# Two-slab products of 512 columns in the up and down stages, and down products in two passes of eight tiles

## The reference

```python
def conv_ffn(h, w_up, conv_w, conv_b, w_down):          # w_up 2048 x 11264, w_down 5632 x 2048
    u = causal_dwconv(h @ w_up, conv_w, conv_b)         # three taps along the tokens
    g, val = jnp.split(u, 2, axis=-1)
    return (jax.nn.silu(g) * val) @ w_down
...
x = x + gate_f * conv_ffn(h, w_up, conv_ffn_w, conv_ffn_b, w_down)
```

## Time and profile before

| | us |
|---|---|
| median of three runs | 2589.81 (2589.5 to 2592.26) |
| the profiled execution | 2596.39 |
| its span, first to last instruction | 2594.7 |
| PE busy | 2421.5 (93% of the span) |
| DVE busy | 1869.9 (72%) |
| ACT busy | 1129.7 (44%) |
| granted PE clock, mean | 0.97 of 2.4 GHz |
| moved by DMA | 615.73 MB, 237 GB/s |

### The profile page before, as it was taken

The page is one execution under the profiler, slowest core; times in us unless marked ns, Lnnn a source line. Parts: engine busy times, 40 slices in busy tenths (PEclk is TensorE's granted clock), DMA queues, the critical chain, the costliest instruction groups (busy, mean ns, idle before and its releaser), DMA issues.

```text
span 2594.7 us, 51150 instructions
## 1 busy us (share of the span) xinstructions
PE 2421.5 (93%) x21498; PEld 2357.6 (91%) x21498; DVE 1869.9 (72%) x2202; ACT 1129.7 (44%) x1246; POOL 96.1 (4%) x184
## 2 busy tenths in 40 slices
PE   4899958899999999999899889999999999999997
PEld 4899848799999999999799788888999999999997
DVE  6988878888777677777788666668877554555645
ACT  3344363355543334443543344433554443344433
POOL 0020000000000000000000000000000000000000
PEclk8999979899999999999999999899999999999999
DMA  8988947777778877779478122218576455555552
GB/s 356 421 333 320 352 160 270 281 267 263 281 284 308 327 277 265 284 275 344 176 272 320 67 89 97 97 65 308 213 281 250 178 181 192 178 179 183 188 212 97
DMA packets 88526, 615.73 MB, mean 237 GB/s; under 512 B 9656, under 2 KB 13264, under 8 KB 14928
## 3 DMA queue, kind: packets, MB, share of 16 engines
q1 hardware_dynamic: 65216, 445.07, 45.9%
q0 software_dynamic: 23184, 168.83, 17.2%
HBM read 609.64 MB, written 4.22 MB: 237 GB/s over the span
## 4 chain that ended last, share of the span: by engine, by line
PE 74%; DVE 14%; DMA 5%; ACT 5%; issue 2%; SPq 0%; DVEq 0%; POOLq 0%; ACTq 0%
PE ps L742 22%; PE ps L744 22%; PE ps L743 22%; DMA ada_raw<-in_ada_stream 3%; DVE ada_raw L1651 2%; DVE first_raw L1651 2%; DVE w_lo L1639 2%; DVE w_lo L1635 1%; DMA first_raw<-in_ada_stream 1%; ACT w_hi L1109 1%; PE ps L628 1%; DMA w_raw<-in_w_stream 1%; PE ps L654 1%; DVE xbc L1786 1%; PE ps L779 1%
## 5 line engine op out<-in xcount | busy, mean ns | idle before, releaser
L742 PE MATMUL ps<-h_hi,w_hi 128*128 128x256 f32 x4480 | 1284.6, 287 | 78.6 <-DVE h_lo L1767 34.1
L743 PE MATMUL ps<-h_lo,w_hi 128*128 128x256 f32 x4480 | 1275.5, 285 | 0.0
L744 PE MATMUL ps<-h_hi,w_lo 128*128 128x256 f32 x4480 | 1274.8, 285 | 0.0
L742 PEld LDWEIGHTS ps<-h_hi,w_hi 128*128 128x128 f32 x4480 | 867.8, 194 | 89.7 <-DVE h_lo L1767 36.1
L1635 DVE TENSOR_TENSOR w_lo<-w_raw,w_hi 128x2048 fp32r<-128x2048 f32 x297 | 678.8, 2288 | 309.9 <-ACT w_hi L1103 309.6
L743 PEld LDWEIGHTS ps<-h_lo,w_hi 128*128 128x128 f32 x4480 | 868.0, 194 | 0.5
L744 PEld LDWEIGHTS ps<-h_hi,w_lo 128*128 128x128 f32 x4480 | 867.8, 194 | 0.0
L1103 ACT CAST w_hi<-w_raw 128x2048 fp32r<-128x2048 f32 x298 | 567.6, 1908 | 678.0 <-DMA w_raw<-in_w_stream 665.7
L1651 DVE SCALAR_TENSOR_TENSOR ada_raw<-ada_raw,ada_c 128x2048 f32<-128x2048 f32 x160 | 365.3, 2285 | 42.6 <-DMA ada_raw<-in_ada_stream 42.4
L742 PE MATMUL ps<-hid_hi,w_hi 128*128 (+1 forms) x1344 | 377.3, 281 | 7.1 <-DVE w_lo L1635 5.5
L744 PE MATMUL ps<-hid_hi,w_lo 128*128 (+1 forms) x1344 | 375.7, 280 | 0.0
(11 more groups left out here) (353 smaller groups left out, 1581.4 us busy)
## 6 DMA issues: line engine op xcount, KB each, us to landing
w_raw<-in_w_stream SPq DMA_DIRECT2D x372, 1024.0 KB, 5.3
ada_raw<-in_ada_stream POOLq DMA_DIRECT2D x160, 1024.0 KB, 7.2
first_raw<-in_ada_stream SPq DMA_DIRECT2D x32, 1024.0 KB, 10.1
kept_raw<-in_w_stream SPq DMA_DIRECT2D x4, 1024.0 KB, 9.4
x<-in_x_t SPq DMA_DIRECT2D x1, 2048.0 KB, 9.9
cs_b<-cs_rows SPq DMA_DIRECT2D x4, 512.0 KB, 6.8
x_kept<-x SPq DMA_DIRECT2D x1, 2048.0 KB, 14.7
out_t<-x SPq DMA_DIRECT2D x4, 512.0 KB, 2.7
```

Source lines behind the costliest of these rows:

```text
L742: mm(o, hi, r_hi, start=first, stop=False, **kw)
L743: mm(o, hi, r_lo, start=False, stop=False, **kw)
L744: return mm(o, lo, r_hi, start=False, stop=last, **kw)
```

## The change

The two halves of an activation become slabs of one tensor (`h_both`, `hid_both`). A new helper `wide` replaces `three` in the up and down stages: one matmul of the high weights with both slabs, 512 columns, fills the whole bank (hi*hi left, hi*lo right), and a second one of the low weights with the high slab, 256 columns, adds lo*hi to the right half. Whoever reads a result must add the two halves of a bank. In the up stages, ACT first copies the four right halves to `tmp` (`small`), DVE adds the left halves (`add`) and both give the banks back; the taps read `tmp`. One step more stands in each chunk's order.

A down output tile now fills a bank, so eight of the 16 tiles fit, and the down product runs in two passes. A unit is two k-tiles (256 rows) by 1024 columns (`_down_units`, laid out on the host). Eight tiles are ended in the middle of the stage and eight at its end, bank by bank (`down_tile`), and DVE adds each to `x` in two steps, left and right half (`down_add`). The squares of the first eight tiles follow the middle of the second down stage. In the first down stage one ada sum goes with each of the units 2 to 10 and 15 to 23; in the second one the counts stand in the call. PE's loop over the down units is unrolled. The diff, cut to its core (the helpers replaced stand above; the calls of the second block are changed alike, and the order of buffers in SBUF too):

```diff
+            sb(under, "before_prob_t_a", [P, KT, T])
             prob_t_a = sb(under, "prob_t", [P, 4, 384])
-        h_lo = sb(ctx, "h_lo", [P, KT, T], F32R)
+        h_both = sb(ctx, "h_both", [P, 2, KT, T], F32R)
+        h_hi, h_lo = h_both[:, 0], h_both[:, 1]
...
+            hid_both = sb(s, "hid_both", [P, 2, 2 * FFN_A, T], F32R)
+            hid_hi, hid_lo = hid_both[:, 0], hid_both[:, 1]
...
+
+            first = 4 * (e_next % 2)
+            return [(first + j) % 8 for j in range(8)]
...
+            def wide(b, hi, lo, k, first, both=h_both, big=h_hi):
+                mm(ps[:, b, :].rearrange("p (a t) -> p a t", a=2), hi, both[:, :, k], start=first, stop=False,
+                   skip_group_check=True)
+                return mm(ps[:, b, T:512], lo, big[:, k], start=False, stop=False, skip_group_check=True)
...
-                        elif kind == "cols" and added is not None and i == 0:
+                        elif kind == "wide" and added is not None and i == 0:
                             for j in range(4):
-                                pe.wait_ge(down_evac, added + j + 1)
+                                pe.wait_ge(down_out, 16 * added + 8 + j + 1)
                                 for k in range(4):
                                     w = slice(k * 512 + j * P, k * 512 + j * P + P)
-                                    last = three(bank(4 * par_ + j), w_h[:, w], w_l[:, w], h_hi[:, k], h_lo[:, k],
-                                                 k == 0, False)
+                                    last = wide(4 * par_ + j, w_h[:, w], w_l[:, w], k, k == 0)
...
+            def down(d, u0, hc0, e_next, n, name=None):
...
+                banks, per = down_banks(e_next), n // 2
...
+                def tile(b, w_h, w_l, f0, first):
+                    for f in range(2):
+                        w = slice(f * 1024 + b * P, f * 1024 + b * P + P)
+                        last = wide(b, w_h[:, w], w_l[:, w], f0 + f, first and f == 0, hid_both, hid_hi)
+                    return last
+
...
-                                         hid_lo[:, i], i == 0 and j % 2 == 0, False, skip_group_check=True)
+                    for q in range(2):
+                        pe.wait_ge(hid_lo_s, hc0 + q + 1)
+                        w_h, w_l = weights(q)
+                        for b in banks[4 * half:4 * half + 4]:
...
-                with pe.Fori(1, n // 4 - (name is not None)) as b:
-                    body(b)
+                for q in range(2, n):
...
+                    w_h, w_l = weights(q)
+                    for k, b in enumerate(banks):
+                        if q == per:
+                            pe.wait_ge(down_out, 16 * d + k + 1)
+                        last = tile(b, w_h, w_l, f0, q == per)
+                        if q in (per - 1, n - 1):
+                            last.then_inc(down_tile, 1)
+                        if q == per and k == 0:
+                            pe.wait_ge(down_tile, 16 * d + 8)
+                            pe.nop().then_inc(units_used, 1)
+                    if q == n - 1:
+                        pe.wait_ge(down_tile, 16 * d + 16)
+                        pe.nop().then_inc(units_used, 1)
+                    elif q != per - 1:
+                        last.then_inc(units_used, 1)
...
             def sums(name, n):
...
+                def small(c, par_):
+                    chunk_done(c, u0)
+                    nc.scalar.copy(tmp[:], ps[:, 4 * par_:4 * par_ + 4, T:512]).then_inc(act_evac, 1)
+
                 def taps(c, par_):
-                    chunk_done(c, u0)
+                    act.wait_ge(dve_evac, c + (e0 + 3))
                     for i in range(4):
                         o = 16 * c + 4 * i + 16 * (hc0 % (FFN_A + FFN_B))
-                        last = A(conv_y[:, par_, i], bank(4 * par_ + i), ACT.Identity, bias=pc(par_name, o + 3),
+                        last = A(conv_y[:, par_, i], tmp[:, i], ACT.Identity, bias=pc(par_name, o + 3),
                                  scale=pc(par_name, o + 2))
-                    last.then_inc(act_evac, 1)
+                    last.then_inc(S("conv_open"), 1)
...
+                    if u_next is not None:
+                        hi_unit(u_next)
+                        hi_unit(u_next + 1)
+                    for k in range(8, 16):
+                        down_squares(d, name, joint, k, banks[k - 8])
...
+                def up(c, par_):
+                    lo(c, 0, u0)
+                    lo(c, 1, u0)
+                    evac[0](c - 1, 1 - par_)
+                    some_ada(c, 2, (par_ - e0) % 2)
+                    lo(c, 2, u0)
+                    evac[1](c - 1, 1 - par_)
+                    some_ada(c, 3, (par_ - e0) % 2)
+                    evac[2](c - 1, 1 - par_)
+                    lo(c, 3, u0)
+                    evac[3](c - 1, 1 - par_)
...
+                def add(c, par_):
+                    dve.wait_ge(act_evac, c + (e0 + 3))
+                    tt(tmp[:], ps[:, 4 * par_:4 * par_ + 4, 0:T], tmp[:], ALU.add).then_inc(dve_evac, 1)
+
                 def taps(c, par_):
-                    dve.wait_ge(act_evac, c + (e0 + 3))
+                    dve.wait_ge(S("conv_open"), c + (hc0 + 1))
...
-                            last = stt(out=conv_y[:, par_, i, d:T], in0=ps[:, 4 * par_ + i, 0:T - d],
+                            last = stt(out=conv_y[:, par_, i, d:T], in0=tmp[:, i, 0:T - d],
...
+            def down_add(d, gate0, k, banks):
+                for e in (k, k + 1):
+                    dve.wait_ge(down_tile, 16 * d + e + 1)
+                    b = banks[e % 8]
+                    j = 8 * (e // 8) + b
+                    stt(out=x[:, j], in0=ps[:, b, 0:T], scalar=mod[:, gate0 + j:gate0 + j + 1], in1=x[:, j], op0=ALU.mult,
+                        op1=ALU.add).then_inc(down_half, 1)
+                for e in (k, k + 1):
+                    dve.wait_ge(down_half, 16 * d + e + 1)
+                    b = banks[e % 8]
+                    j = 8 * (e // 8) + b
+                    stt(out=x[:, j], in0=ps[:, b, T:512], scalar=mod[:, gate0 + j:gate0 + j + 1], in1=x[:, j], op0=ALU.mult,
+                        op1=ALU.add).then_inc(down_out, 1)
...
+            def down(d, u0, n, gate0, p0, products, e_next, u_next=None, name=None, joint=0):
+                banks, per = down_banks(e_next), n // 2
+                pair = p0
+                for q in range(2, n - 2 if name is not None else n):
+                    if name is not None and q >= n - 4:
+                        lo_kept(name, q - n + 4)
+                    if q == per + 1:
+                        for k in range(0, 8, 2):
+                            down_add(d, gate0, k, banks)
+                    lo_unit(u0 + q)
+                    if name is not None and per + 2 <= q < per + 6:
+                        for k in (2 * (q - per - 2), 2 * (q - per - 2) + 1):
+                            if k:
+                                add_square(name, joint, k)
+                    if q in products:
+                        for _ in range(products[q]):
+                            ada(pair, pair % 2)
+                            pair += 1
...
+                elif u_next is not None:
+                    lo_unit(u_next)
+                for k in range(8, 16, 2):
+                    if name is not None and u_next is not None and k == 12:
+                        lo_unit(u_next + 1)
+                    down_add(d, gate0, k, banks)
+                    if name is not None:
+                        for e in (k - 2, k - 1):
+                            if e >= 8:
+                                add_square(name, joint, e)
+                if name is None:
+                    lo(0, 1, u_next)
+                dve.wait_ge(down_out, 16 * d + 16)
...
+                if pairs:
+                    ada(2 * c + (98 - 18), 0)
                 lo(c, 2, U_UP1A)
                 ev[1](c - 1, 1 - par_)
                 if pairs:
-                    ada(2 * c + (98 - 18), 0)
+                    ada(2 * c + (99 - 18), 1)
+                ev[2](c - 1, 1 - par_)
                 lo(c, 3, U_UP1A)
-                ev[2](c - 1, 1 - par_)
-                if pairs:
-                    ada(2 * c + (99 - 18), 1)
+                ev[3](c - 1, 1 - par_)
...
+            mod_bias(GATE_F, KT)
+            down(0, U_DN1A, 2 * FFN_A, GATE_F, 104, {**{q: 1 for q in range(2, 11)}, **{q: 1 for q in range(15, 24)}}, UP1B, U_UP1B)
...
+            down(1, U_DN1B, 2 * FFN_B, GATE_F, 142, {2: 1, 3: 2, 4: 1, 5: 1, 6: 1, 7: 1, 8: 1, 14: 1, 15: 1, 16: 1, 17: 1}, C_LORA, U_LORA,
+                 "mid", 2)
...
+            steps.link(ts(mu1[:], pcol("mu", 0, 27), -1.0, 1.0, ALU.mult, ALU.add))
+            dve.nop().then_inc(S("mu1"), 1)
...
 
+def _down_units(w):
+
+    k, n = w.shape
```

272 lines of the change are left out of this document (103 added, 169 removed).

## The result

The changed kernel takes 2577.9 us (median of 9 runs, 2567.5 to 2588.6) where the kernel before, run beside it, takes 2592.3 (2587.3 to 2597.5): ratio 0.9946, 95% interval 0.9924 to 0.9967, some 14 us faster. The forecast was 32.3 us faster, 2557.5 us: the sign is right and the time lies in the range, but less than half of the gain came. The profiled execution took 2577.89 us, span 2576.2.

A forecast was written before the change was run, and what follows sets the result against it. TensorE (PE), busy 93% of the span, was taken to bound the kernel. Gains of 49.1 us less losses of 16.8 gave net 32.3, from 2589.8 to 2557.5 us; range 2543 to 2584.

The forecast's parts named there:

- Part 1: Up and down products: two matmuls replace three, 0.3468 us an up pair; 37.2 us gained up, 7.3 down.
- rival d: Down stages: the short matmul spacing stays with wide matmuls, giving 2550 us; chance 0.15.
- Rival (a): Up and down products: the two-slab operand costs like two matmuls, 0.2400 us; slower, 2601.5 us; chance 0.06.
- Rival (a'): Only part of the third matmul's cost is saved, wide steps about 0.2344 us; no change, 2590 us; chance 0.03.
- Part 2: Up chunks' longer hand-over: low weights still arrive in time, slack 1.2 us; nothing lost.
- rival (b): Up chunks with ada sums: DVE becomes the bound, up to 26 us per us short, 2583.5 us; chance 0.11.
- Part 3: Four hand-overs from up to down: PE waits longer for unit 2's low weights, 2.5 us each, 9.9 lost.
- Part 4: Down stages in two passes: bank additions hidden, some stalls go, while ada loads, tails and moved constants cost time.
- The start of the next up stage: Behind the first down stages: the wait of 1.3 us, twice, shrinks to some 0.4; 1.8 us gained.
- The ada loads: Down stages: denser loads cost 1 us in the first and 3 us in the second, bounds 0 and 10.
- Rival (c): Down stages: the ada loads hold them back by 10 us instead of 4, giving 2564 us; chance 0.10.
- Tails: Ends of the second down stages: PE waits longer for DVE's additions and squares before the sums; 2.4 us lost.

The follow-up runs named there:

- contiguous: The changed kernel with the two slabs interleaved, so the 512 moving columns lie in one piece; 2572.6 us, ratio 0.9914 to the kernel before.
- split512: The changed kernel with each 512-column matmul issued as two of 256 columns, a weight load each; 2606.0 us, ratio 1.0042 to the kernel before.
- early_spread: early_unit with the eight ada sums of the second down stage's first half given one to a unit; 2561.5 us, ratio 0.9883.
- early_unit: The changed kernel with the next down stage's unit 2 weights (high and low) made ahead of the last up chunk's product; 2566.4 us, ratio 0.9891.
- bank_runs: early_spread with an up unit's pairs ordered four in a row into one bank, then the next bank; 2562.8 us, ratio 0.9888.
- up_only_early: up_only with unit 2's high and low weights for the next down stage made ahead of the product; 2564.0 us, ratio 0.9891.
- after: The changed kernel itself, in its first measurement and profile; 2577.9 us, ratio 0.9946 to the kernel before.
- after_again: The changed kernel without any edit, run once more with a new profile; 2576.5 us, ratio 0.9932 to the kernel before.
- small_first: The changed kernel with each pair's matmuls in the other order, 256 columns first and 512 after; 2575.2 us, ratio 0.9924.
- k_outer: The changed kernel with the first weight unit of both second up stages done row tile by row tile; 2581.1 us, ratio 0.9952.
- up_only: The kernel before with wide matmuls in the up products alone, down stages as they were; 2570.5 us, ratio 0.9924.

## Why the prediction was right or wrong

**Part 1, the pair: mechanism right, size off.** The step that failed is "A new pair takes 0.2268 + 0.1200 = 0.3468 us", priced at 37.2 us over the up stages: these saved 26.3 where 36.7 were forecast. I took it from one short stretch of matmuls all of one size and one pace of 256-column matmuls, and asked only for the two-slab operand's cost, bounded from 0.2268 to 0.2400. A mixed stream has two paces, and the long one costs 0.8 us in the first and 4.3 in each second up stage: 9.4 of the 11.8 us missing. That the short pace meets 0.3468 is in part luck: it is made of 0.230 and 0.117, two terms that are off in opposite directions. And the prediction's own sign of being wrong, a wide step above 0.23, did come: in the long pace the wide steps are 233 to 241 ns, 237 in the mean. The earlier trace rows had shown 256-column matmuls at 0.1163 to 0.1175 beside 0.1200; I noted that the cause of it was not visible and bounded only a gain from it (rival d), where it called for a loss as well.

Rival (a) is out by contiguous and split512. Rival (a'), wide steps of about 0.2344 and no gain at all, is out as to the time; but as to the pair it is what the long pace is, 0.3533 against its 0.3544, and half of the third matmul's cost was saved there. The Trainium skill's gap of N/2.4 + 2.5 ns ("TensorE: Matmul & The Clock Gate", Back-to-back issue gap), which the page gives for a matmul without a budget for its weight load and by which a third matmul costs 2.5 ns, does not agree with this stream, where every matmul has a load: between split512 and the unedited kernel 32 us lie on 4224 triples, 7.6 ns each. In the down stages the pair took 346.7 against 350.0 to 353.3, some 8.0 us where I had 7.3.

**Part 2, no stall in the up chunks: right but for one step.** In the chunk that starts at 628.5 us the low weights of unit 3 come from 641.54:

```profile
629.78 1.23 DVE L1974 TENSOR_TENSOR tmp<-ps,tmp 128x1024 f32<-128x1024 f32 x1 [1.84 <-ACT tmp L1308]
...
641.54 2.28 DVE L1656 TENSOR_TENSOR w_lo<-w_raw,w_hi 128x2048 fp32r<-128x2048 f32 x1
```

They end 15.3 us after the boundary (walked: 15.4), and the addition takes 1.23 (estimated: 1.22). At one chunk boundary the low weights were late, behind two ada sums in a row:

```profile
715.24 4.49 DVE L1656 TENSOR_TENSOR w_lo<-w_raw,w_hi 128x2048 fp32r<-128x2048 f32 x2
...
717.58 0.50 PE L750 MATMUL ps<-h_both,w_hi 128*128 128x512 f32 x1
```

That step took 0.41 us in place of 0.12; the first of the two subtractions in DVE's row ends at about 717.5, and early_spread's row of this place, shown above, names the wait. A wait for low weights inside the up chunks was named as a sign of being wrong; here it is 0.3 us, once. As the cost that rival (b) meant it is out. The rival's price was set for 26 chunks with two ada sums; the trace has 30 (24, 20 and 16 sums in three stages), so a us too little in each would have cost 30.

**Part 3, the junction: the place and the wait right, the cost too small, for what follows the stall was left out.** Forecast 2.5 us each. PE after, at the second down stage:

```profile
1160.05 0.28 PE L752 MATMUL ps<-hid_both,w_lo 128*128 128x256 f32 x1
1163.46 0.47 PE L750 MATMUL ps<-hid_both,w_hi 128*128 128x512 f32 x1 [3.13 <-DVE w_lo L1660]
...
1165.06 0.63 PE L750 MATMUL ps<-hid_both,w_hi 128*128 128x512 f32 x1
...
1165.70 0.63 PE L750 MATMUL ps<-hid_both,w_hi 128*128 128x512 f32 x1
```

From 1160.05 to 1163.46 are 3.41 us in place of 0.12; before, such a step was 0.61 to 0.66. So 2.7 us each, 11.0 in all against 9.9. But from 1164.7 to 1168.2 the granted clock is at 1.2 GHz: a pair takes 0.64 instead of 0.35, and 3.4 us of that cost 1.6. The clock fell at three of the four junctions, the third time for 5.7 us of work, 5.7 us of cost in all that I had nothing for. early_unit confirms the place: with the stalls away, the three down stages that got no new one were 2.4 to 6.0 us shorter than in the two profiles of the unedited kernel, and the median fell by 10 us although a new stall of 6 came in the fourth.

**Part 4, the down stages.** The start of the next up stage: 0.69 us from last to first matmul against 1.4, 1.4 us gained in all (1.8 forecast). The stalls at 816.7 and 1257.3 are gone as forecast, 3.3 us. The ada loads cost nothing in the first down stage and 0.5 us in the second (stalls of 1.4, 0.5 and 1.4 us in place of one of 2.8), where I had 4.0: the loads landed in 7.1 us, not later than before, but faster. Rival (c) is out for this kernel; early_unit shows how near it was. Tails: PE is idle 5.34 us before the mid sums (5.7 forecast) and 2.22 before the last; with the constants 1.4 us lost, 2.9 forecast. All terms of the down stages: 8.0 + 1.4 + 3.3 - 0.5 - 1.4 - 11.0 - 5.7 = -5.9, against -5.8 in the table and -4.4 forecast; that the forecast is near is luck, owed to the clock's cost standing against ada loads and tails that cost less than I gave them.

**The time itself.** Of the 18 us by which the measured gain (14.4) falls short of the forecast one (32.3), 11.8 are in the changed stretches. The other 6 are within what the unchanged part does from run to run (517 to 527 us in the profiles of this kernel), and I can't put them to a cause.

## What to carry to other kernels

A step between two matmuls, read in one stretch of equal ones, is a value with a band, not a price: look in how many paces the same instruction stream runs over a whole trace, and put that band on every term that is multiplied by thousands. A stall is dearer than its length where the granted clock falls with it. When a hand-over gets longer, look in the trace for work on the same engines that the waiting engine needs next and that could go ahead of it: making one weight unit earlier was worth 10 us here, the whole change 14 to 20. And take a change apart before keeping all of it: the part with the most code, two passes over the down products, is worth 1.4 to 5.2 us by the stages of three profiles and does not show in the medians; the best kernels here (early_spread 0.9883, bank_runs 0.9888, early_unit and up_only_early 0.9891, not told apart by their intervals) share the wide up products and the early unit.

## What the hardware showed that I had not expected

An alternating stream of 512- and 256-column matmuls, each with a new weight tile, ran at 346.7 or at 353.3 ns a pair for hundreds of pairs at the same full clock, and in these profiles it changed between them only behind a gap. Where a stall put 3.1 to 3.5 us between two matmuls of a stage that is otherwise full, the granted clock went to 1.2 GHz for 3.4 to 6.8 us in 19 of 28 places (after, after_again, contiguous, split512, small_first, k_outer, up_only), from 1.1 us before PE started again to 1.3 us after; in early_spread and the kernels built on it, which have no such stall, it did not fall while the down products ran. And one matmul fewer for the same columns was worth between 3.3 ns (down, 350.0 to 346.7) and 13.3 ns (up, 360.0 to 346.7).
